# Adaptive-norm weights in 256-column tiles, c loaded transposed, and GpSimd's constant loads without a wait

## The reference

```python
mod = jax.nn.silu(c) @ w_ada[l] + b_ada[l]          # c [1024], w_ada [1024, 6144]
sh1, sc1, gt1, sh2, sc2, gt2 = jnp.split(mod, 6, axis=-1)
h = rms_norm(x, g_pre_mix[l]) * (1 + sc1) + sh1
y = hybrid_mixer(h, w_in[l], ...)                   # w_in [1024, 2320]; window attention and gated linear attention
x = x + gt1 * rms_norm(y, g_post_mix[l])
h = rms_norm(x, g_pre_ffn[l]) * (1 + sc2) + sh2
y = moe_ffn(h, ...)                                 # 32 experts, the four best of each token
x = x + gt2 * rms_norm(y, g_post_ffn[l])
```

## Time and profile before

| what | value |
|---|---|
| median of 3 runs | 3081.45 us (3080.64 to 3082.95) |
| the profiled execution: its own time | 3080.64 us |
| its span, first to last instruction | 3078.8 us |
| TensorE matmul busy | 2795.1 us, 91% |
| VectorE busy | 1427.5 us, 46% |
| ScalarE busy | 922.2 us, 30% |
| GpSimd busy | 220.9 us, 7% |
| mean granted TensorE clock | 0.938 |

### The profile page before, as it was taken

One profiled execution on the slowest core, in us unless ns is written; L12 is line 12 of the kernel. 1 busy time (PEld: TensorE's weight loads), 2 busy tenths in 40 slices (PEclk: granted clock), 3 DMA queues, 4 the chain that ended last, 5 costly groups with the idle time before them and its releaser, 6 DMA issues. The chain is left out here.

```text
span 3078.8 us, 41584 instructions
## 1 busy us (share of the span) xinstructions
PE 2795.1 (91%) x17494; PEld 2007.4 (65%) x17494; DVE 1427.5 (46%) x2005; ACT 922.2 (30%) x1201; POOL 220.9 (7%) x160
## 2 busy tenths in 40 slices
PE   6856999999999999959248998999999999999998
PEld 5635434434434433429238988989889989898897
DVE  3464122122122222234766766566566575574655
ACT  3323111010101011123325544444443443435433
POOL 2000000000000000000000001005311020012200
PEclk8967899999999999979569999999999999998999
DMA  8613599999999999965004555545546656450463
GB/s 285 227 72 123 212 375 416 376 378 417 417 353 401 416 374 382 416 244 189 4 27 155 186 174 185 201 151 173 196 155 206 200 169 198 158 166 30 151 200 115
DMA packets 292711, 713.73 MB, mean 232 GB/s; under 512 B 15587, under 2 KB 189369, under 8 KB 259430
## 3 DMA queue, kind: packets, MB, share of 16 engines
q1 hardware_dynamic: 281168, 690.27, 60.7%
q10 hardware_dynamic: 9734, 17.02, 1.7%
q0 software_dynamic: 1616, 3.70, 0.4%
HBM read 709.90 MB, written 1.05 MB: 231 GB/s over the span
## 5 line engine op out<-in xcount | busy, mean ns | idle before, releaser
L369 DVE TENSOR_TENSOR lo<-ring,hi 128x2048 fp32r<-128x2048 f32 x251 | 602.4, 2405 | 305.4 <-ACT hi L360 305.2
L360 ACT ACTIVATE hi<-ring 128x2048 fp32r<-128x2048 f32 x251 | 475.8, 1898 | 200.3 <-PE bank L638 131.0
L1728 PE MATMUL bank<-expert,xg 128*64 128x512 f32 x2304 | 522.2, 598 | 0.0
L430 PE MATMUL bank<-x_hi,hi 128*128 128x256 f32 x1568 | 382.8, 285 | 0.0
L430 PE MATMUL bank<-x_lo,hi 128*128 128x256 f32 x1568 | 380.2, 281 | 0.0
L1728 PEld LDWEIGHTS bank<-expert,xg 128*64 128x64 f32 x2304 | 157.6, 137 | 310.9 <-issue 309.8
L430 PEld LDWEIGHTS bank<-x_lo,hi 128*128 128x128 f32 x1568 | 295.9, 189 | 2.5 <-issue 1.0
L430 PEld LDWEIGHTS bank<-x_hi,hi 128*128 128x128 f32 x1568 | 295.0, 188 | 3.3 <-issue 1.6
L1825 DVE TENSOR_TENSOR acc<-bank,acc 128x512 f32<-128x512 f32 x144 | 89.4, 683 | 407.7 <-PE bank L1815 407.5
L1798 PE MATMUL bank<-expert,aT 128*64 128x512 f32 x1152 | 254.9, 595 | 1.1 <-DMA expert<-in_w_mlp 1.0
L1753 DVE TENSOR_SCALAR sx<-bank 128x256 f32<-128x256 f32 x72 | 30.2, 420 | 393.8 <-PE bank L1739 393.3
(11 more groups left out here) (618 smaller groups left out, 3927.2 us busy)
## 6 DMA issues: line engine op xcount, KB each, us to landing
expert<-in_w_mlp SPq DMA_DIRECT2D x384, 1024.0 KB, 11.6
ring<-in_l_ffn_w_in SPq DMA_DIRECT2D x88, 1024.0 KB, 5.1
ring<-in_l_ffn_w_out SPq DMA_DIRECT2D x44, 1024.0 KB, 4.9
ring<-in_w_ada SPq DMA_DIRECT2D x24, 1024.0 KB, 6.8
ring<-in_l_gm_w_in SPq DMA_DIRECT2D x24, 1024.0 KB, 5.2
ring<-in_ffn_w_up SPq DMA_DIRECT2D x22, 1024.0 KB, 5.1
ring<-in_w_in SPq DMA_DIRECT2D x21, 1024.0 KB, 5.3
ring<-in_l_gm_w_out SPq DMA_DIRECT2D x12, 1024.0 KB, 4.9
```

Source lines behind the costliest of these rows:

```text
L360: e.activation(k.half("hi", u), k.slot(j), ACT.Copy).then_inc(*k.up("hi_done"))
L369: e.tensor_tensor(k.half("lo", u), k.slot(k.units[u][0]), k.half("hi", u).bitcast(F32), SUB).then_inc(*k.up("lo_done"))
L430: e.matmul(o, l, r, start=fresh, stop=False, skip_group_check=True)
L1728: i = e.matmul(banks[n][j][h * CAP:(h + 1) * CAP, :], x, W[:, (2 * h + j) * 512:(2 * h + j + 1) * 512], start=c == 0, stop=False, skip_gro ...
```

## The change

- c is loaded straight as 128 x 8, so that partition p holds elements 8p to 8p + 7. The transpose, its bank and the wait for the identity ahead of it go; tanh on ScalarE and silu on VectorE move to the start programs. To fit, the row blocks of w_ada are also taken as rows 8p + k.
- w_ada is worked in 24 tiles of 256 columns. A tile is one load of 1 MB, with eight pieces of 1 KB for each partition, and eight products. The first stage does eight tiles, the transposes of x stand after the sixth, the levels have two steps per tick, and the window attention has one step at each of its five ticks.
- ScalarE issues x ahead of the identity.
- GpSimd's loads no longer wait.
- `wup` and `ga` have memory of their own, and the row tiles are half as wide.

```diff
-            tick(1 if li - 1 < 6 else 0)
+            tick(2 if li - 1 < 6 else 0)
...
-            tick(1 if li < 6 else 0)
+            tick(2 if li < 6 else 0)
...
 def start_act(k, e):
     A, t, n = k.A, k.t, 128
-    e.dma_start(t["c"], flat_param(A, "c").rearrange("(k p) -> k p", p=128)).then_inc(*k.up("c_in", by=16))
+    e.dma_start(t["c"], flat_param(A, "c").rearrange("(p k) -> p k", p=128)).then_inc(*k.up("c_in", by=16))
+    e.dma_start(t["xa"], A["x"][0].rearrange("(b p) n -> p b n", p=128)).then_inc(*k.up("x_in", by=16))
     e.dma_start(t["const"][:, 0:n], A["const_f"][:, 0:n]).then_inc(*k.up("ident_in", by=16))
-    e.dma_start(t["xa"], A["x"][0].rearrange("(b p) n -> p b n", p=128)).then_inc(*k.up("x_in", by=16))
     params_load(k, e, 0)
+    e.wait_ge(*k.total("c_in"))
+    e.activation(t["sc"], t["c"], ACT.Tanh, scale=0.5).then_inc(*k.ACT("c"))
...
 def start_pool(k, e):
     A, t, n = k.A, k.t, 128
-    e.wait_ge(*k.mm("ada", 2, 1))
     e.dma_start(t["wup"], A["w_gla_gate_up"][0]).then_inc(*k.up("const_in", by=16))
...
 def ada_units(k, which):
-
-    W = wview(k.A["w_ada"][0])
     for i in which:
-        for h in range(2):
-            k.raw(("ada", i, h), W[:, 4 * h:4 * h + 4, i * 512:(i + 1) * 512], 4, 512, "mm_done", "ada", i, h)
+        k.raw(("ada", i), k.A["w_ada"][0].rearrange("(p k) n -> p k n", p=128)[:, :, i * 256:(i + 1) * 256], 8, 256, "mm_done", "ada", i)
...
 def ada_pe(k, e, i):
+    u, landed = k.raw_at(("ada", i))
     bank = k.bank(e, "ada", i)
-    for h in range(2):
-        u, landed = k.raw_at(("ada", i, h))
-        e.wait_ge(*landed)
+    e.wait_ge(*landed)
+    for c0 in range(0, KC, 4):
         for q in range(4):
-            c = 4 * h + q
-            t = e.matmul(bank[32 * q:32 * q + 32, :], k.t["sc"][:, c:c + 1].to_broadcast([128, 32]), u[:, q, :], start=h == 0, stop=h == 1, skip_group_check=True)
-        t.then_inc(*k.MM("ada", i, h))
+            t = e.matmul(bank[32 * q:32 * q + 32, 0:256], k.t["sc"][:, c0 + q:c0 + q + 1].to_broadcast([128, 32]), u[:, c0 + q, :],
+                         start=c0 == 0, stop=c0 > 0, skip_group_check=True)
+    t.then_inc(*k.MM("ada", i))
...
-    for j in range(4):
-        t = e.matmul(k.mod_bank[:, 4 * i + j:4 * i + j + 1], row[:, j * 128:(j + 1) * 128], k.t["pick"][:, 0:1])
+    for j in range(2):
+        t = e.matmul(k.mod_bank[:, 2 * i + j:2 * i + j + 1], row[:, j * 128:(j + 1) * 128], k.t["pick"][:, 0:1])
...
-ROW_TILES = {4: ("g1", 0), 5: ("g1", 1), 10: ("g2", 0), 11: ("g2", 1)}
+ROW_TILES = {8 + j: ("g1", j) for j in range(4)}
+ROW_TILES.update({20 + j: ("g2", j) for j in range(4)})
...
 def first_pe(k, e):
     k.mod_bank = k.bank(e, "mod", hold=True)
-    e.wait_ge(*k.total("ident_in"))
-    e.wait_ge(*k.total("c_in"))
-    e.transpose(k.bank(e, "c")[:, 0:KC], k.t["c"], k.cc("ident")[0:KC, 0:KC]).then_inc(*k.MM("c"))
     e.wait_ge(*k.dve("c"))
-    for i in range(4):
+    for i in range(8):
         ada_pe(k, e, i)
         if i == 0:
+            e.wait_ge(*k.total("ident_in"))
             params_pe(k, e, 0)
         else:
             flip_pe(k, e, i - 1)
-        if i == 2:
+        if i == 5:
             turn_rows_pe(k, e, "pre1")
-    flip_pe(k, e, 3)
+    flip_pe(k, e, 7)
...
-    for n in ("row0", "row1"):
-        k.sb(n, [128, 512], F32, c)
-    k.t["wup"], k.t["ga"] = k.t["g2"][0:16, 0:256], k.t["g2"][0:16, 256:512]
+    for n, parts in (("wup", 16), ("row0", 128), ("row1", 128)):
+        k.sb(n, [parts, 256], F32, c)
```

More of the change, by code:

```diff
@@ L1063, in flip_pe @@
     if i in ROW_TILES:
-        bank = k.bank(e, "gate", i)
+        bank = k.bank(e, "grow", i)
         e.wait_ge(*k.act("ada", i))
-        e.matmul(bank[:, :], k.t["pick"], row).then_inc(*k.MM("flip", i))
+        e.matmul(bank[:, 0:256], k.t["pick"], row).then_inc(*k.MM("flip", i))
         return
     e.wait_ge(*k.act("ada", i))
-    for j in range(4):
-        t = e.matmul(k.mod_bank[:, 4 * i + j:4 * i + j + 1], row[:, j * 128:(j + 1) * 128], k.t["pick"][:, 0:1])
+    for j in range(2):
+        t = e.matmul(k.mod_bank[:, 2 * i + j:2 * i + j + 1], row[:, j * 128:(j + 1) * 128], k.t["pick"][:, 0:1])
     t.then_inc(*k.MM("flip", i))
@@ L1076, in ada_act @@
         e.wait_ge(*k.mm("flip", i - 2))
-    e.wait_ge(*k.mm("ada", i, 1))
-    e.activation(k.t[f"row{i % 2}"], k.got("ada", i)[:, :], ACT.Copy).then_inc(*k.ACT("ada", i, frees=("ada", i)))
-    k.past("act", ("ada", i, 1))
+    e.wait_ge(*k.mm("ada", i))
+    e.activation(k.t[f"row{i % 2}"], k.got("ada", i)[:, 0:256], ACT.Copy).then_inc(*k.ACT("ada", i, frees=("ada", i)))
+    k.past("act", ("ada", i))
 def gate_row_act(k, e, i):
@@ L1084, in gate_row_act @@
     e.wait_ge(*k.mm("flip", i))
-    e.activation(k.t[n][:, j * 512:(j + 1) * 512], k.got("gate", i)[:, :], ACT.Copy).then_inc(*k.ACT("grow", i, frees=("gate", i)))
-ROW_TILES = {4: ("g1", 0), 5: ("g1", 1), 10: ("g2", 0), 11: ("g2", 1)}
+    e.activation(k.t[n][:, j * 256:(j + 1) * 256], k.got("grow", i)[:, 0:256], ACT.Copy).then_inc(*k.ACT("grow", i, frees=("grow", i)))
+ROW_TILES = {8 + j: ("g1", j) for j in range(4)}
+ROW_TILES.update({20 + j: ("g2", j) for j in range(4)})
 class Ticks:
     def __init__(self, k, e, step):
-        self.k, self.e, self.step, self.next = k, e, step, 4
+        self.k, self.e, self.step, self.next = k, e, step, 8
     def __call__(self, n):
-        for _ in range(min(n, 13 - self.next)):
+        for _ in range(min(n, 25 - self.next)):
             self.step(self.k, self.e, self.next)
@@ L1105, in ada_next_pe @@
 def ada_next_pe(k, e, i):
-    if i == 4:
+    if i == 8:
         e.wait_ge(*k.dve("mod", 0))
-    if i < 12:
+    if i < 24:
         ada_pe(k, e, i)
-    if i > 4:
+    if i > 8:
         flip_pe(k, e, i - 1)
 def ada_next_act(k, e, i):
-    if i < 12:
+    if i < 24:
         ada_act(k, e, i)
@@ L1132, in first_pe @@
             flip_pe(k, e, i - 1)
-        if i == 2:
+        if i == 5:
             turn_rows_pe(k, e, "pre1")
-    flip_pe(k, e, 3)
+    flip_pe(k, e, 7)
 def first_act(k, e):
-    e.wait_ge(*k.mm("c"))
-    e.activation(k.t["sc"], k.got("c")[:, 0:KC], ACT.Tanh, scale=0.5).then_inc(*k.ACT("c"))
     rms_act(k, e, "pre1", lambda b, h: k.total("x_in"))
-    for i in range(4):
+    for i in range(8):
         ada_act(k, e, i)
@@ L1148, in first_dve @@
     t = k.t
[L1149 to L1152, removed]
     rms_dve(k, e, "pre1")
     params_dve(k, e, 0)
-    e.wait_ge(*k.mm("flip", 3))
+    e.wait_ge(*k.mm("flip", 7))
     e.tensor_tensor(t["mod"][:, 0:16], k.mod_bank[:, 0:16], k.V["b_ada"][:, 0:16], ADD).then_inc(*k.DVE())
@@ L1158, in first_dve @@
     e.scalar_tensor_tensor(t["s1"], t["mod"][:, 8:16], 1.0, k.V["g_pre_mix"], ADD, MUL).then_inc(*k.DVE("mod", 0))
-    k.past("dve", ("ada", 3, 1))
+    k.past("dve", ("ada", 7))
     e.wait_ge(*k.dve())
@@ L1327, in gla_norm_dve @@
     t = k.t
-    row_gate_dve(k, e, "g1", "g1_in", 5)
+    row_gate_dve(k, e, "g1", "g1_in", 11)
     heads_dve(k, e, "glan", 4, t["rr"])
@@ L1388, in swa_dve @@
                       sink=t["sinks"][:, 4 * gi:4 * gi + 4])
-    k.past("dve", ("ada", 11, 1))
-    e.wait_ge(*k.mm("flip", 9))
+    k.past("dve", ("ada", 23))
+    e.wait_ge(*k.mm("flip", 19))
     e.tensor_tensor(t["mod"][:, 24:40], k.mod_bank[:, 24:40], k.V["b_ada"][:, 24:40], ADD).then_inc(*k.DVE(frees=("mod",)))
@@ L1393, in swa_dve @@
     e.scalar_tensor_tensor(t["s2"], t["mod"][:, 32:40], 1.0, k.V["g_pre_ffn"], ADD, MUL).then_inc(*k.DVE())
-    row_gate_dve(k, e, "g2", "g2_in", 11)
+    row_gate_dve(k, e, "g2", "g2_in", 23)
     meet(k, e, DVE_, "mixer", 3)
@@ L1472, in lay_block1 @@
     sb("b1", 2 * NE, 2048)
-    sb("sc", 128, KC), sb("c", KC, 128), sb("mod", 128, 48)
+    sb("sc", 128, KC), sb("c", 128, KC), sb("mod", 128, 48)
     for n in ("s1", "s2"):
@@ L1476, in lay_block1 @@
     sb("g1", 128, DM), sb("g2", 128, DM)
-    ada_units(k, range(4))
+    ada_units(k, range(8))
     with ExitStack() as c:
@@ L1500, in lay_mixer @@
         bi("gq", 128, 2, 256), bi("gk", 128, 2, 256), bi("g", 128, 2, 256)
[L1501 removed]
+        bi("gv", 128, 2, 4, 128), bi("gg", 128, 4, 256), bi("ga", 16, 256)
         bi("S", 128, 4, 3, 128), bi("og", 128, 4, 256)
@@ L1518, in lay_mixer @@
             bi(f"swaout{i}", 128, 512)
-        ada_units(k, range(4, 12))
+        ada_units(k, range(8, 24))
     k.sb("mo_hi", [128, KC, 256], F32R, c)
```

3 lines of the change are left out of this document (added).

## The result

| | median | range of the runs |
|---|---|---|
| before | 3081.45 us | 3079.50 to 3082.95 (5) |
| after | 3098.48 us | 3095.97 to 3104.08 (5) |

The ratio is 1.0058, with a 95% interval of 1.0044 to 1.0074: slower, by 17.0 us. The prediction had the sign, but 3089.2 us with a range up to 3094.5, so the loss is about twice the forecast one (+7.8) and lies 4 us outside the range. The profiled execution took 3097.4 us with a span of 3095.5, 16.7 more than before; the mean clock is the same, 0.938.

What follows compares the result with a forecast made beforehand. DMA was taken to bound the start, waits for w_ada the decay levels, VectorE's chain the attention. First stage +4.7, levels +1.0 and attention +2.1 made +7.8 us, a median of 3089.2 us, range 3081.5 to 3094.5.

Steps and rivals of the forecast that it cites:

- the price of the pieces: First stage: w_ada pieces shrinking from 2 KB to 1 KB cost 0 us, as w_in's 1 KB pieces land 2.7 us apart.
- loads slower everywhere: Rival: 1 KB pieces take 3.1 us a load, +3 and +4 us, about 3096; inside a 0.11 chance shared with unseen waits.
- w_in's pace: Ground against slower loads: w_in's third and fourth loads, in 1 KB pieces, land 2.7 us apart, as 2 KB pieces do.
- Levels: Decay levels: scores wait for ScalarE's copy behind the next Exp, 5.4 us per level; +1.0 us, bounds -0.5 and +3.
- Constants ahead of a7: First stage: GpSimd's 3.70 MB, queued from 0.5 us, delay the eighth w_ada load from 28.0 to 43.5 us.
- both of those rivals: Constants yield to SP's queue (-7.7 us, chance 0.06); constants cost only their bytes, small packets hiding (+1.8 to +4.3, chance 0.22).
- a7 to m_hi: First stage: m_hi starts 2.8 us behind the eighth w_ada load's landing, where it was 6.1 us.
- under the loads: First stage: the 16 transposes come two tiles earlier, under the loads, and no longer stand between the last load and m_hi.
- What the wait for w1 swallows: First stage: most of m_hi's 12.2 us delay vanishes in the old wait for the second w_in load, leaving +4.7 us.
- Attention: Window attention up to mo_hi: a gain at its start, then a last tick behind everything; +2.1 us, bounds 0 and +3.
- The tail: End of window attention: flip, copy and VectorE's two g2 operations (1.23 us each) stand uncovered behind the last head output.
- The gain at the first tick: Start of window attention: 8 products of 256 columns take 0.9 us instead of 3.64, so VectorE starts 2.3 us sooner.

Runs made afterwards that it cites:

- after_gpsimd_waits: The changed kernel with GpSimd's loads held behind the sixth w_ada load, as before the change: 3092.07 us, 1.0035 of the kernel before.
- before_gpsimd_behind_w4: The kernel before with GpSimd's loads held back until the sixth w_in load is split: 3070.19 us, 0.9971 of the kernel before.
- before_gpsimd_at_once: The kernel before with only GpSimd's wait left out, w_ada staying in 512-column tiles of 2 KB pieces: 3085.87 us, 1.0018 of the kernel before.
- after_flip_two_back: The changed kernel with a third row tile and each flip in the levels a step later: 3096.08 us, 1.0047 of the kernel before.
- before_256_columns: The kernel before with 256-column w_ada tiles and two steps a tick, old rows, c path and GpSimd wait: 3092.65 us, 1.0036 of the kernel before.

## Why the prediction was wrong

**The term that failed is the price of the pieces, put at 0.** From a step of 2.7 us between w2 and w3 I took it that pieces of 1 KB land as fast as those of 2 KB. But w2 and w3 had both been under way together (w3 for 11.9 us), so this was the distance of two ends and not the time of a load. after_gpsimd_waits has next to nothing beside the loads from 14 to 24 us, and there they take 3.0 us; so do w_in's own loads, 349 GB/s and 3.0 us apart in before_gpsimd_behind_w4. At a7 the new tiles cost 3.8 us (31.8 for 28.0), of which 2.4 are eight times 0.3. The rival "loads slower everywhere" had 3.1 us, +3 and +4, and came out at 3096, the nearest of all to 3098.5; I had it inside 0.11. Its ground against, "w_in's pace", is that same pair of rows. But its +3 in the levels is not shown to be the loads' time, as told under Levels below. The Trainium skill (DMA: Bandwidth & Descriptors, "Why small descriptors are slow") counts a fixed part for each packet, and the trace agrees in kind; the estimate by it, 4% a load, is under the 11% that the windows show.

**Constants ahead of a7: right in kind, and the exact size is luck.** 15.5 us were forecast for GpSimd's bytes. Their measured price is 13.7 in the kernel before, 1.8 under the forecast, and 47.3 - 31.8 = 15.5 in the changed one. They do not yield and do not hide: both of those rivals are out. But the 15.5 hold a part that is no byte of GpSimd's. The first three loads come late, at 22.1, 29.4 and 31.5 us, and then TensorE sets the pace: a tile each 2.8 us (35.03, 37.84), and SP issues a4 to a7 at 31.4, 34.2, 37.0 and 39.8, as the products three tiles before end. From 30 to 34 us the DMA engines have too little to do, 219 GB/s where they move 349 from 26 to 30; an estimate from these is 4 x 130 / 349 = 1.5 us. The eight products take 1.93 us there and 1.07 from 46.69 on. The windows print a clock of 1.00, but 1.94 is what they take at a granted 0.50 (199.18). From 1 to 24 us the queues moved as follows, in the changed kernel (GpSimd's is q0, SP's q1):

```profile
q0 software_dynamic: 1225, 3.63, 52.7%
q1 hardware_dynamic: 1721, 1.75, 32.1%
```

and in before_gpsimd_at_once:

```profile
q0 software_dynamic: 735, 3.48, 45.9%
q1 hardware_dynamic: 1474, 2.95, 40.1%
```

By 24 us GpSimd's queue has brought nearly all of its 3.70 MB in both. SP's has moved 1.75 MB with pieces of 1 KB, and 2.95 with pieces of 2 KB. So small pieces also get less of a shared engine. That the queues take turns by packets is how I read it; no run tests it alone.

**a7 to m_hi** took 3.6 us, not 2.8. The transposes, put two tiles earlier "under the loads", ran from 43.38 to 46.8, and a6 (44.3) and a7 (47.3) had landed around them; their products stood behind. TensorE was busy for 13.97 of the 14 us from 36 to 50, so there was no time under the loads for the transposes to use.

**What the wait for w1 swallows: right.** 12.2 us at m_hi were to become 4.7, so 7.5 were to vanish; in after 16.8 became 8.4, in before_gpsimd_at_once 11.0 became 3.0. So the two parts of the first stage should cost more together than each alone, as the second finds the slack used up; the profiled executions say so (3.0 and -1.4 alone, 8.4 together). The medians do not: 5.4 and 11.6 add up to 17.0. The profiled execution of after_gpsimd_waits was 4 us shorter than the median of its kernel, so this is not settled.

**Levels: +4.0 for +1.0.** The mechanism is as forecast. In the first cycle TensorE waits 3.54 us for the copy behind the Exp; the cycle takes 7.84 us, and 7.3 were forecast (119.61, the first difference before, to 126.9). Four cycles take 5.2 to 5.3 us for 5.4. The miss is the fourth cycle, 8.54 us for 5.4, and the forecast had two things there at nothing. One is late loads: ahead of the cycle's scores TensorE waits 0.81 and 1.36 us for w_ada. The other is the clock: from 149 to 155 us 0.50 is granted, the second tile's products take 1.93 us for 1.07 and the scores 2.24 for 1.26. The forecast had the low clock in the first cycle alone. The loads' slower pace is not simply added: over the levels TensorE waits 2.2 us for w_ada in the changed kernel and 7.6 in the one before, and the DMA share is 0.83 for 0.93. No run parts the load from the clock, so how the 3.0 us divide stays open.

Between 134 and 138 us DMA ran nearly dry (share 0.31 and 0.18, windows of after), as two slots of the ring come free close together behind the Exp:

```profile
134.00:136.00 2.00, 2.00 (x26) 1.23 (x24) 1.68 (x5) 0.00 (x0) 0.00 (x0) 0.73 0.31 105
136.00:138.00 2.00, 1.75 (x22) 0.71 (x18) 0.57 (x1) 1.37 (x3) 0.00 (x0) 1.00 0.18 50
```

**Attention: +3.0 for +2.1.** The tail is as forecast, 3.97 us from the last head output to mo_hi for 0.93 before: 3.0 for 2.9. The gain at the first tick was to be 2.3 us and is 0.9: VectorE starts 5.02 us after TensorE's first product, for 5.89 before. I took the 16 records of the row at 3.64 for 16 products; they are two for each, so the work was halved and not quartered, and it takes 1.94, not 0.9.

Put together, with 3.8 for the new tiles at a7, 0.8 at m_hi, the 3.0 by which the levels missed and 0.9 in the attention, the forecast of +7.8 becomes +16.3; the marks show 8.4 + 4.0 + 3.0 = 15.4, and 16.7 with the 1.3 behind mo_hi. The sum has 9.3 for the first stage, where 8.4 was measured. Only the first of these terms is shown by runs of its own (a7 at 31.8, 32.2 and, with the old rows and c, 32.7 us); the others are read from the trace of the changed kernel.

## What to carry to other kernels

Loads on another queue aren't free because nobody waits for them: they take their bytes' time and more from the load that is urgent, so place them by what else is under way, and look again at who is late after each move, and whether anybody needs it (here w1, then w3 and w4, then w8, which TensorE did not miss). Take the time of a load from a stretch in which the queue is full and alone, never from the distance between two landings that shared the wait; and check how many records make one instruction before dividing a row's time. A stall that is about to vanish hides only one delay: sum the delays of all parts first, then subtract it. And when a stretch got longer, look at TensorE's granted clock there before blaming the loads.

## What the hardware showed that I hadn't expected

- Pieces of 1 KB against 2 KB: 348 against 387 GB/s with DMA engines full, 3.0 against 2.7 us for 1.05 MB, for w_ada and w_in alike (349 GB/s). Whether the rows follow one another over partitions or inside one (371 GB/s at 2 KB) matters less.
- The first load of SP's queue, issued 0.5 us ahead of GpSimd's first, took 21.4 us beside them; w4 took 20.9 and 22.4 us in the runs with GpSimd behind w2's split, and w8 21.6 us in the one behind w5's.
- P x V of a job of the window attention: 3.65 us at a granted clock of 0.50, 1.93 in the kernel where 235 to 240 us has 0.84. One step moved to an earlier tick went with this; what moved the clock no run tests.
- A cycle of the levels with two tiles took 5.32 and 5.16 us at a granted 1.00 (the second and third of the changed kernel), and 7.78 us at 0.50 with TensorE busy throughout (after_flip_two_back and before_256_columns).
